# Stick-breaking attention on one Trainium2 core: the suffix sums of log keeps as two passes of rounded fp32 in place of one of plain fp32

## The chip, the cores and the metric

One core of one Trainium2 chip runs the whole program. The metric is device time in microseconds (us), the lower the better. The kernel before takes 2057.86 us (median of 3 runs, 2056.94 to 2059.09).

## The reference, cut to what matters

The program computes four transformer layers of 256 tokens and width 1024. Each layer is an FFN, a mixer and another FFN. The mixers are one retention, one latent attention (MLA) and two of the kind that the change touches, here called stick sublayers (the last two layers). A stick mixer projects the token rows to q, k, v (8 heads of 64), three convolution inputs and one pooling input, and its attention is

```python
z = einsum('bhqd,bhkd->bhqk', q_blk, kh) * scale
mask = k_pos[None, :] < q_pos[:, None]
log_keep = where(mask, log_sigmoid(-z), 0.0)
between = cumsum(log_keep, axis=3, reverse=True) - log_keep
a = where(mask, exp(log_sigmoid(z) + between), 0.0)
out = einsum('bhqk,bhkd->bhqd', a, vh)
```

Since log_sigmoid(z) = z + log_sigmoid(-z), the exponent is z plus the suffix sum of the log keeps, the key's own included: that sum is what the kernel forms on TensorE.

## The kernel before, in words

**Weights.** All projections read weights through a ring of three slots of 128x2048 fp32 (1 MB). SyncE loads slot n when `low(n-3)` is done. ScalarE's `high(n)` rounds it into `w_hi` (L881), and VectorE's `low(n)` puts the remainder into `w_lo` (L1197). TensorE then makes three matmuls of type fp32r (rounded fp32) per 128x128 tile: high by high, high by low, low by high (L400 to L402; L473 for the output projections). `high(n)` needs its slot loaded and `slot_done` of slot n-3; `low(n)` needs `high(n)`; TensorE's `take(n)` needs `low(n)`.

**Order.** There is no planner. Each engine has one list of instructions, written by hand, which it runs in order; what comes from another engine is waited for on a semaphore. An instruction that waits holds up all that stands behind it on its engine.

**Stick sublayer.** Ten weight slots (b to b+9) give q, k, v and the rest, and four give the output projection. The 8 heads go in 4 pairs s = 0 to 3. A pair's scores are kept transposed, keys on partitions; only the causal part stands, 384 columns per head (256 queries for the first 128 keys, 128 for the second). The steps of a pair, each with its engine:

- TensorE `pair_logits` (L731, L732): z in plain fp32 into the banks of `down[0]`.
- ScalarE `pair_log` (L1143, L1145, L1148): |z|, exp(-|z|), ln(1 + that).
- VectorE `pair_keep` (L1524, L1527): max(z, 0) plus that, then times the negated mask: `z_lk`, the log keeps of both heads, 128x768.
- TensorE `pair_sums` (L749 to L753), for each of two heads: z again for the first keys (L749), a triangle of ones times the log keeps on top (L750), all ones times those of the second keys (L751), and z and triangle for the second keys (L752, L753). All in plain fp32; each plain fp32 matmul stands as two instructions in the trace.
- VectorE `pair_min` (L1512), ScalarE `pair_exp` (L1131): the attention weights.
- TensorE `pair_out` (L763, L764), ScalarE `pair_high` (L1135), VectorE `pair_low` (L1517): the output, split for the next projection.

TensorE's list around them (L779 to L808): half of slot b+4, `pair_logits(0)`, the other half, slot b+5, `pair_sums(0)`, `pair_logits(1)`, slot b+6, `pair_out(0)`, half of slot b+7, `pair_sums(1)`, `pair_logits(2)`, the other half, `pair_out(1)`, slot b+8, `pair_sums(2)`, `pair_logits(3)`, slot b+9, `pair_out(2)`, `pair_sums(3)`, the pooling matmuls (L806), output projection. ScalarE's list is at L1150 to L1179 (`slot_out(j)` copies a projection out, L939) and VectorE's at L1530 to L1567. GpSimd makes the pooling sums (L1661 to L1666) at the same time. L513 and L438 are the transposes and the first matmuls after a sublayer's norm.

Of the kernel before, what the change touches and what calls it, by code (L numbers as in the profile page):

```python
# [17 lines left out]
P = 128  # L18
S = 256
# [15 lines left out]
CAUSAL = 384  # L35
# [62 lines left out]
def build(nc, ins, out):  # L98
# [3 lines left out]
    with ctx:  # L102
# [95 lines left out]
        sm = sb("sm", [P, 2, 2, 4])  # L198
        c_hi, c_lo = h_hi[:, 0:3, :], h_lo[:, 0:3, :]
        hgain = sb("hgain", [P, TOK])  # L200

        bank0, bank1 = ps("bank0", 512), ps("bank1", 512)
        down = [ps("down0", 1024), ps("down1", 1024)]
# [33 lines left out]
        c_turned, c_hi_done, c_lo_done = sem("c_turned"), sem("c_hi_done"), sem("c_lo_done")  # L237
        uq_mm, uq_out, ukv_mm, ukv_out = sem("uq_mm"), sem("uq_out"), sem("ukv_mm"), sem("ukv_out")
        qk_ready, qk_turned, qk_T = sem("qk_ready"), sem("qk_turned"), sem("qk_T")
        s_z, s_abs, s_ln, s_lk = sem("s_z"), sem("s_abs"), sem("s_ln"), sem("s_lk")  # L240
        s_cs, s_min, s_exp, s_out, s_hi, s_lo = (sem(n) for n in ("s_cs", "s_min", "s_exp", "s_out", "s_hi", "s_lo"))
        conv_done, conv_hi, conv_lo = sem("conv_done"), sem("conv_hi"), sem("conv_lo")
# [13 lines left out]
        def wait(eng, s, value):  # L256

            if value > 0:
                eng.wait_ge(s, value)
# [126 lines left out]
        def _(pe):  # L386
# [220 lines left out]
            for u, kind in enumerate(SUBLAYERS):  # L607
# [115 lines left out]
                else:  # L723
# [14 lines left out]

                    def pair_sums(s):

                        pe.wait_ge(s_lk, c0 + s + 1)
                        wait(pe, s_min, c0 + s)
                        tri, ones = cst("tri"), cst("ones")
                        for g in range(2):
                            o = 64 * g
                            k, q = s_k[o:o + 64, s, :], s_q[o:o + 64, s, :]
                            lk = z_lk[:, g, :]
                            first, second = mid[2 + g][:, 0:S], mid[2 + g][:, S:CAUSAL]
                            mm(first, k[:, 0:P], q, start=True, stop=False)  # L749
                            mm(first, tri, lk[:, 0:S], start=False, stop=False)  # L750
                            mm(mid[2 + g][:, P:S], ones, lk[:, S:CAUSAL], start=False, stop=True)  # L751
                            mm(second, k[:, P:S], q[:, P:S], start=True, stop=False)  # L752
                            last = mm(second, tri, lk[:, S:CAUSAL], start=False, stop=True)  # L753
                        last.then_inc(s_cs, 1)

                    def pair_out(s):
# [80 lines left out]
        def _(sc):  # L837
# [32 lines left out]
            def high(n, at=None, base=None):  # L870

                m = n if at is None else at
                if at is None:
                    sc.wait_ge(raw_in[n % RING], 16 * (n // RING + 1))
                    wait(sc, slot_done, n - RING + 1)
                else:
                    i, n0 = base
                    sc.wait_ge(raw_in[n0 % RING], i * 16 + 16 * (n0 // RING + 1))
                    sc.wait_ge(slot_done, m - RING + 1)
                r = n % RING  # L880
                act_fn(w_hi[:, r, :], raw[:, r, :], ACT.Copy).then_inc(hi_ready, 1)  # L881
# [109 lines left out]
            for u, kind in enumerate(SUBLAYERS):  # L991
# [44 lines left out]
                else:  # L1036
                    if kind == "ret":
                        mem = mem_heads(0)

                        def pair_high(p):  # L1040
                            sc.wait_ge(m_turned, p + 1)
                            act_fn(m_hi[:, 2 * p:2 * p + 2, :], (bank6, bank7)[p % 2][:, :].rearrange("p (k t) -> p k t", k=2),
                                   ACT.Copy).then_inc(m_hi_done, 1)
# [72 lines left out]
                    else:  # L1116
# [4 lines left out]
                        def slot_out(j):  # L1121
                            copy_out(b + j, places[j], scale=AD ** -0.5 if j in (2, 5) else 1.0)
# [14 lines left out]
                        def pair_log(s):  # L1137

                            sc.wait_ge(s_z, c0 + s + 1)
                            z = down[0][:, :].rearrange("p (a b) -> p a b", a=2)[:, :, 0:CAUSAL]  # L1140
                            if s:
                                sc.wait_ge(s_exp, c0 + s)
                            act_fn(z_abs, z, ACT.Abs).then_inc(s_abs, 1)  # L1143
                            sc.wait_ge(s_abs, 3 * (c0 + s) + 1)
                            act_fn(z_abs, z_abs, ACT.Exp, scale=-1.0).then_inc(s_abs, 1)  # L1145
                            sc.wait_ge(s_abs, 3 * (c0 + s) + 2)
                            wait(sc, s_lk, c0 + s)
                            act_fn(z_ln, z_abs, ACT.Ln, bias=1.0).then_inc(s_abs, 1)  # L1148

                        pair_log(0)  # L1150
                        slot_out(4)
                        high(b + 7)
                        slot_out(5)
                        high(b + 8)
# [1 line left out]
                        pair_log(1)  # L1156
                        slot_out(6)
                        pair_high(0)
                        high(b + 9)
                        pair_exp(1)  # L1160
                        pair_log(2)
                        slot_out(7)
                        high(b + 10)
                        pair_high(1)
                        slot_out(8)
# [2 lines left out]
                        pair_log(3)  # L1168
                        slot_out(9)
                        pair_high(2)  # L1170
                        high(b + 12)
                        pair_exp(3)
                        sc.wait_ge(small_in, SMALL_FIRST + SMALL_STICK * (sticks + 1))
                        sc.wait_ge(pool_mm, sticks + 1)
                        for j in range(2):
                            act_fn(m_hi[:, 6 + j, :], bank0[:, j * S:(j + 1) * S], ACT.Copy, scale=small[:, j, 3:4]).then_inc(pool_hi, 1)
                        sc.wait_ge(conv_done, 2 * (sticks + 1))
# [11 lines left out]
        def _(ve):  # L1189
            v = nc.vector  # L1190
# [16 lines left out]
            def pre_scale(p, t):  # L1207

                ve.wait_ge(pre_in, 16 * (p + 1))
                ve.wait_ge(pre_rs, 2 * p + t + 1)  # L1210
                for c in range(2):
                    h = slice(c * 512, (c + 1) * 512)
                    wait(ve, turned, 4 * (p - 1) + 2 * t + c + 1)
                    v.scalar_tensor_tensor(xn[:, t, h], (mem_rows if p == 0 else x)[:, t, h], stat[:, 4 + t:5 + t],  # L1214
                                           (post_gain if p == 0 else pre_gain)[:, h], ALU.mult, ALU.mult).then_inc(pre_xn, 1)
# [93 lines left out]

            for t in range(T):  # L1310
                pre_scale(0, t)
            pre_low(0, 0)
            low(0)
            low(1)
# [12 lines left out]
            for u, kind in enumerate(SUBLAYERS):  # L1327
# [47 lines left out]
                else:  # L1375
# [126 lines left out]
                    else:  # L1502
# [16 lines left out]
                        def pair_keep(s):  # L1519
# [7 lines left out]
                                last = v.tensor_tensor(z_lk[:, g, :], z_ln[:, g, :], cst("negmask"), ALU.mult)  # L1527
                            last.then_inc(s_lk, 1)

                        pair_keep(0)  # L1530
                        low(b + 7)
                        pair_min(0)
                        low(b + 8)
                        pair_keep(1)
                        pair_low(0)
                        pair_min(1)
                        low(b + 9)
                        pair_keep(2)
                        low(b + 10)
                        pair_low(1)  # L1540
                        pair_min(2)
                        low(b + 11)
                        pair_keep(3)
                        pair_low(2)

                        def convolve(j):

# [149 lines left out]
```

## Time and profile before

| what | value |
|---|---|
| median of 3 runs | 2057.86 us (2056.94 to 2059.09) |
| span of the profiled execution | 2058.1 us; no other time is listed for it |
| TensorE (PE) matmul busy | 1980.5 us, 96% |
| VectorE (DVE) busy | 1087.5 us, 53% |
| ScalarE (ACT) busy | 957.1 us, 47% |
| GpSimd (POOL) busy | 139.7 us, 7% |
| mean granted TensorE clock | 0.993 of full speed |
| DMA | 356.46 MB, mean 173 GB/s |

The span is one execution, from its first to its last instruction. Matmuls are pipelined, so successive starts, not the durations, say what one costs. A timeline row gives the start, the duration, the engine, the line and the count of merged instructions; the brackets give the idle time before it and what ended that.

### The profile page before, as it was taken

To read this page: it belongs to the slowest core of one execution; us is meant where nothing else is said; L and a number is where in the kernel's file an instruction comes from. 1 tells how busy PE (TensorE), PEld (TensorE's weight loads), DVE (VectorE), ACT (ScalarE), POOL (GpSimd) and SP (SyncE) were. 2 spreads that over 40 slices of the span, in tenths; PEclk is the share of its full clock that TensorE was granted. 3 is DMA by queue.
4 is the path that set the end of the run, shared out by engine and by line. 5 is a ranking of instruction groups with operands and counts; after the bars stand their busy time and mean duration, and the time that the engine had idled before them with its cause. 6 is when DMAs were issued, how large, how long until landed. Compare 5 with 4: busy or idle time off the path is not lost.

```text
span 2058.1 us, 32564 instructions
## 1 busy us (share of the span) xinstructions
PE 1980.5 (96%) x13724; PEld 1832.0 (89%) x13724; DVE 1087.5 (53%) x990; ACT 957.1 (47%) x1097; POOL 139.7 (7%) x149
## 2 busy tenths in 40 slices
PE   7999999999999998999999999999999999999998
PEld 6999899899899986899989998889998998988997
DVE  4644656644554456544564445554446445456444
ACT  5445554533543356533453346553445335555443
POOL 2500022000000000000000002000000000200000
PEclk9999999999999999999999999999999999999999
DMA  8655543555465542455555555355555554535552
GB/s 286 205 183 184 168 154 129 199 187 185 146 214 188 188 148 81 162 186 183 184 185 184 183 165 184 103 174 190 187 164 194 186 189 147 185 103 174 184 185 101
DMA packets 261987, 356.46 MB, mean 173 GB/s; under 512 B 8976, under 2 KB 230544, under 8 KB 261904
## 3 DMA queue, kind: packets, MB, share of 16 engines
q1 hardware_dynamic: 258304, 342.15, 50.4%
q0 software_dynamic: 3600, 13.11, 2.1%
q8 instruction: 63, 1.03, 0.2%
q14 instruction: 20, 0.16, 0.0%
HBM read 354.19 MB, written 1.05 MB: 173 GB/s over the span
## 4 chain that ended last, share of the span: by engine, by line
PE 87%; DVE 6%; issue 3%; ACT 3%; DMA 1%; POOL 0%; SPq 0%; DVEq 0%; POOLq 0%; ACTq 0%
PE down L473 24%; PE bank L400 17%; PE bank L402 17%; PE bank L401 17%; PE bank L447 2%; PE bank L513 2%; DVE upd L1234 2%; ACT junk L852 1%; PE bank L438 1%; PE bank L439 1%; DVE w_lo L1203 1%; DVE xn L1214 1%; DVE x L1240 1%; DMA raw<-in_ffn_w_gu 1%; PE down L749 0%
## 5 line engine op out<-in xcount | busy, mean ns | idle before, releaser
L1197 DVE TENSOR_TENSOR w_lo<-raw,w_hi 128x2048 fp32r<-128x2048 f32 x300 | 687.8, 2295 | 522.9 <-ACT w_hi L881 522.9
L400 PE MATMUL bank<-h_hi,w_hi 128*128 128x256 f32 x2944 | 835.6, 284 | 0.0
L401 PE MATMUL bank<-h_lo,w_hi 128*128 128x256 f32 x2944 | 833.0, 283 | 0.0
L402 PE MATMUL bank<-h_hi,w_lo 128*128 128x256 f32 x2944 | 833.0, 283 | 0.0
L881 ACT ACTIVATE w_hi<-raw 128x2048 fp32r<-128x2048 f32 x322 | 614.2, 1908 | 263.8 <-PE down L473 201.4
L400 PEld LDWEIGHTS bank<-h_hi,w_hi 128*128 128x128 f32 x2944 | 564.7, 192 | 6.4 <-issue 2.5
L401 PEld LDWEIGHTS bank<-h_lo,w_hi 128*128 128x128 f32 x2944 | 564.8, 192 | 2.5
L402 PEld LDWEIGHTS bank<-h_hi,w_lo 128*128 128x128 f32 x2944 | 564.8, 192 | 0.0
L473 PE MATMUL down<-w_hi,m_hi 128*128 128x512 f32 x832 | 267.2, 393 | 0.0
L473 PE MATMUL down<-w_lo,m_hi 128*128 128x512 f32 x832 | 264.7, 390 | 0.0
L473 PE MATMUL down<-w_hi,m_lo 128*128 128x512 f32 x832 | 264.4, 389 | 0.0
L473 PEld LDWEIGHTS down<-w_hi,m_lo 128*128 128x128 f32 x832 | 156.2, 188 | 33.2
L473 PEld LDWEIGHTS down<-w_lo,m_hi 128*128 128x128 f32 x832 | 156.3, 188 | 33.0
L1002 ACT ACTIVATE m_hi<-big 128x512 fp32r<-128x512 f32 x80 | 50.3, 629 | 287.8 <-DVE big L1336 287.8
L473 PEld LDWEIGHTS down<-w_hi,m_hi 128*128 128x128 f32 x832 | 151.2, 189 | 27.7 <-issue 1.4
L998 ACT ACTIVATE big<-bank 128x512 f32<-128x512 f32 x88 | 52.6, 598 | 250.2 <-PE bank L402 219.3
L1336 DVE TENSOR_TENSOR big<-bank,big 128x512 f32<-128x512 f32 x88 | 60.9, 692 | 144.6 <-PE bank L402 109.5
L1588 POOL TENSOR_TENSOR stat<-stat,const 128x1 f32<-128x1 f32 x24 | 14.4, 599 | 1506.7 <-ACT stat L863 1506.7
L438 PE MATMUL bank<-w_hi,h_hi 128*128 128x256 f32 x384 | 95.3, 286 | 12.5 <-issue 7.2
L439 PE MATMUL bank<-w_hi,h_lo 128*128 128x256 f32 x384 | 93.9, 282 | 0.0
L438 PEld LDWEIGHTS bank<-w_hi,h_hi 128*128 128x128 f32 x384 | 73.3, 191 | 16.7 <-issue 10.4
L513 PE MATMUL bank<-const,xn 128*128 128x128 f32 x208 | 36.9, 315 | 45.5 <-DVE xn L1214 45.4
(207 smaller groups left out, 1395.1 us busy)
## 6 DMA issues: line engine op xcount, KB each, us to landing
raw<-in_ffn_w_gu SPq DMA_DIRECT2D x88, 1024.0 KB, 5.1
raw<-in_ffn_w_down SPq DMA_DIRECT2D x88, 1024.0 KB, 4.9
raw<-in_ffn_w_gate SPq DMA_DIRECT2D x44, 1024.0 KB, 5.3
raw<-in_ffn_w_up SPq DMA_DIRECT2D x44, 1024.0 KB, 5.4
raw<-in_w_in SPq DMA_DIRECT2D x20, 1024.0 KB, 5.2
raw<-in_ret_w_in SPq DMA_DIRECT2D x13, 1024.0 KB, 5.7
raw<-in_w_o SPq DMA_DIRECT2D x8, 1024.0 KB, 5.0
raw<-in_w_out SPq DMA_DIRECT2D x8, 1024.0 KB, 4.9
```

Source lines behind the costliest of these rows:

```text
L400: mm(o, w_hi[:, r, c:c + P], hi[:, k, :], start=(k == 0), stop=False)
L401: mm(o, w_hi[:, r, c:c + P], lo[:, k, :], start=False, stop=False)
L402: last = mm(o, w_lo[:, r, c:c + P], hi[:, k, :], start=False, stop=(k == KD - 1))
L438: mm(o, hi[:, k, ts], w_hi[:, n % RING, c:c + SC], start=(k == 0), stop=False)
L439: mm(o, lo[:, k, ts], w_hi[:, n % RING, c:c + SC], start=False, stop=False)
L473: last = mm(down[t][:, c * 512:(c + 1) * 512], a[:, k0 + j, ts], w[:, r, j * D + c * 512:j * D + (c + 1) * 512], start=(first and j == 0 a ...
L513: last = tr((bank6, bank7)[c][:, k * P:(k + 1) * P], xn[:, t, (4 * c + k) * P:(4 * c + k + 1) * P], ident)
L881: act_fn(w_hi[:, r, :], raw[:, r, :], ACT.Copy).then_inc(hi_ready, 1)
L998: act_fn(silu_g, bank0[:, :], ACT.Silu).then_inc(silu_done, 1)
L1002: act_fn(m_hi[:, k0:k0 + 2, :], act.rearrange("p (a b) -> p a b", a=2), ACT.Copy).then_inc(act_hi_done, 1)
L1197: v.tensor_tensor(w_lo[:, r, :], raw[:, r, :], w_hi[:, r, :].bitcast(f32), ALU.subtract).then_inc(lo_ready, 1)
L1336: v.tensor_tensor(act, bank1[:, :], silu_g, ALU.mult).then_inc(prod_done, 1)
```

## The change

`pair_sums` gets its triangle and ones in fp32r (`tri_r`, `ones_r`, copied once at the start), and the log keeps as two fp32r tiles, a high part (`lk_hi`, a rounding copy) and a low part (`lk_lo`, the remainder), laid over rows 4 to 6 of `m_hi` and `m_lo`. Per head, the z matmuls stay in plain fp32; the triangle goes over all 384 columns at once, once with each part, and the ones over 128 columns, once with each part. ScalarE gets `keep_high(s)` and VectorE `keep_low(s)`, at the places below. The complete diff:

```diff
@@ build: tiles and semaphores
+        tri_r = sb("tri_r", [P, P], f32r)
+        ones_r = sb("ones_r", [P, P], f32r)
+        lk_hi = m_hi[:, 4:7, :].rearrange("p a b -> p (a b)").rearrange("p (a b) -> p a b", a=2)
+        lk_lo = m_lo[:, 4:7, :].rearrange("p a b -> p (a b)").rearrange("p (a b) -> p a b", a=2)
+        s_lk_hi, s_lk_lo, exact_ready = sem("s_lk_hi"), sem("s_lk_lo"), sem("exact_ready")
@@ TensorE
                     def pair_sums(s):
 
-                        pe.wait_ge(s_lk, c0 + s + 1)
+                        pe.wait_ge(s_lk_lo, c0 + s + 1)
                         wait(pe, s_min, c0 + s)
-                        tri, ones = cst("tri"), cst("ones")
+                        pe.wait_ge(exact_ready, 2)
                         for g in range(2):
                             o = 64 * g
                             k, q = s_k[o:o + 64, s, :], s_q[o:o + 64, s, :]
-                            lk = z_lk[:, g, :]
-                            first, second = mid[2 + g][:, 0:S], mid[2 + g][:, S:CAUSAL]
-                            mm(first, k[:, 0:P], q, start=True, stop=False)
-                            mm(first, tri, lk[:, 0:S], start=False, stop=False)
-                            mm(mid[2 + g][:, P:S], ones, lk[:, S:CAUSAL], start=False, stop=True)
-                            mm(second, k[:, P:S], q[:, P:S], start=True, stop=False)
-                            last = mm(second, tri, lk[:, S:CAUSAL], start=False, stop=True)
+                            z = mid[2 + g][:, 0:CAUSAL]
+                            mm(z[:, 0:S], k[:, 0:P], q, start=True, stop=False)
+                            mm(z[:, S:CAUSAL], k[:, P:S], q[:, P:S], start=False, stop=False)
+                            for lk in (lk_hi, lk_lo):
+                                mm(z, tri_r[:, :], lk[:, g, :], start=False, stop=False)
+                            for part, lk in enumerate((lk_hi, lk_lo)):
+                                last = mm(z[:, P:S], ones_r[:, :], lk[:, g, S:CAUSAL], start=False, stop=(part == 1))
                         last.then_inc(s_cs, 1)
@@ ScalarE
+                        def keep_high(s):
+                            sc.wait_ge(s_lk, c0 + s + 1)
+                            wait(sc, s_cs, c0 + s)
+                            act_fn(lk_hi, z_lk, ACT.Copy).then_inc(s_lk_hi, 1)
+
                         pair_log(0)
                         slot_out(4)
+                        keep_high(0)
                         high(b + 7)
                         slot_out(5)
                         high(b + 8)
@@
                         pair_log(1)
                         slot_out(6)
                         pair_high(0)
+                        keep_high(1)
                         high(b + 9)
                         pair_exp(1)
                         pair_log(2)
                         slot_out(7)
+                        keep_high(2)
                         high(b + 10)
                         pair_high(1)
                         slot_out(8)
@@
                         pair_log(3)
                         slot_out(9)
                         pair_high(2)
+                        keep_high(3)
                         high(b + 12)
                         pair_exp(3)
                         sc.wait_ge(small_in, SMALL_FIRST + SMALL_STICK * (sticks + 1))
                         sc.wait_ge(pool_mm, sticks + 1)
+                        sc.wait_ge(s_cs, c0 + 4)
@@ VectorE, at the start
                 pre_scale(0, t)
+            ve.wait_ge(const_in, 16)
+            v.tensor_copy(tri_r[:, :], cst("tri")).then_inc(exact_ready, 1)
+            v.tensor_copy(ones_r[:, :], cst("ones")).then_inc(exact_ready, 1)
             pre_low(0, 0)
@@ VectorE
+                        def keep_low(s):
+                            ve.wait_ge(s_lk_hi, c0 + s + 1)
+                            v.tensor_tensor(lk_lo, z_lk, lk_hi.bitcast(f32), ALU.subtract).then_inc(s_lk_lo, 1)
+
                         pair_keep(0)
                         low(b + 7)
+                        keep_low(0)
                         pair_min(0)
                         low(b + 8)
                         pair_keep(1)
                         pair_low(0)
+                        keep_low(1)
                         pair_min(1)
                         low(b + 9)
                         pair_keep(2)
                         low(b + 10)
+                        keep_low(2)
                         pair_low(1)
                         pair_min(2)
                         low(b + 11)
                         pair_keep(3)
                         pair_low(2)
+                        keep_low(3)
```

## Rows read from the trace of the kernel before

**Rows 1.** The page's first part and the chain's shares by engine.
```profile
PE 1980.5 (96%) x13724; PEld 1832.0 (89%) x13724; DVE 1087.5 (53%) x990; ACT 957.1 (47%) x1097; POOL 139.7 (7%) x149
...
PE 87%; DVE 6%; issue 3%; ACT 3%; DMA 1%; POOL 0%; SPq 0%; DVEq 0%; POOLq 0%; ACTq 0%
```

**Rows 2.** The waits of TensorE: for what, us in total, times, longest.
```profile
PE down L749 <- DVE big L1527: 0.9, 2, 0.4
```

**Rows 3.** Timeline of TensorE in the first stick sublayer: pair 0, later starts.
```profile
1277.88 0.28 PE L402 MATMUL bank<-h_hi,w_lo 128*128 128x256 f32 x1
1278.09 0.70 PE L749 MATMUL down<-big 64*128 64x256 f32 x2
1278.72 0.70 PE L750 MATMUL down<-big,const 128*128 128x256 f32 x2
1279.25 0.38 PE L751 MATMUL down<-big,const 128*128 128x128 f32 x2
1279.57 0.49 PE L752 MATMUL down<-big 64*128 64x128 f32 x2
1279.98 0.49 PE L753 MATMUL down<-big,const 128*128 128x128 f32 x2
1280.40 0.70 PE L749 MATMUL down<-big 64*128 64x256 f32 x2
...
1282.71 0.71 PE L731 MATMUL down<-big 64*128 64x256 f32 x4
...
1283.57 0.39 PE L400 MATMUL bank<-h_hi,w_hi 128*128 128x256 f32 x1
...
1293.39 0.48 PE L749 MATMUL down<-big 64*128 64x256 f32 x1
...
1308.68 0.48 PE L749 MATMUL down<-big 64*128 64x256 f32 x1
...
1321.42 0.70 PE L749 MATMUL down<-big 64*128 64x256 f32 x2 [0.44 <-DVE big L1527]
```

**Rows 4.** Timeline of TensorE in the MLA sublayer: fp32r matmuls of 384 columns.
```profile
780.31 0.34 PE L417 MATMUL bank<-w_lo,h_hi 128*128 128x384 f32 x1
780.48 0.33 PE L418 MATMUL bank<-w_hi,h_lo 128*128 128x384 f32 x1
```

**Rows 5.** Timeline of VectorE in the first stick sublayer.
```profile
1275.62 1.73 DVE L1527 TENSOR_TENSOR big<-big,const 128x384 f32<-128x384 f32 x2
1277.27 2.28 DVE L1197 TENSOR_TENSOR w_lo<-raw,w_hi 128x2048 fp32r<-128x2048 f32 x1
...
1298.12 1.02 DVE L1512 SCALAR_TENSOR_TENSOR big<-down,const 128x384 f32<-128x384 f32 x2 [6.82 <-PE down L753]
...
1305.05 1.03 DVE L1527 TENSOR_TENSOR big<-big,const 128x384 f32<-128x384 f32 x2
...
1321.80 0.68 DVE L1556 TENSOR_TENSOR big<-big 128x512 f32<-128x512 f32 x1
```

**Rows 6.** Timeline of ScalarE in the first stick sublayer.
```profile
1274.91 1.90 ACT L881 ACTIVATE w_hi<-raw 128x2048 fp32r<-128x2048 f32 x1
...
1299.17 0.85 ACT L1131 ACTIVATE big<-big 128x768 f32<-128x768 f32 x1 [5.24 <-DVE big L1512]
...
1321.05 0.38 ACT L1135 ACTIVATE m_hi<-bank 128x256 fp32r<-128x256 f32 x1 [0.23 <-PE bank L764]
```

**Rows 7.** Timeline of TensorE at the program's start.
```profile
15.63 0.58 PE L438 MATMUL bank<-w_hi,m_hi 128*128 128x256 f32 x1 [2.48 <-ACT w_hi L881]
```

**Rows 8.** Busy time by stretch; columns: length, PE, PEld, DVE, ACT, POOL, PEclk, DMA, GB/s.
```profile
1241.00:1243.00 2.00, 0.45 (x4) 0.25 (x3) 0.99 (x1) 1.84 (x6) 0.54 (x2) 1.00 0.57 198
...
1244.00:1247.00 3.00, 3.00 (x15) 3.00 (x16) 2.80 (x4) 1.38 (x3) 0.53 (x1) 0.50 0.67 232
```

**Rows 9.** Timeline of GpSimd in the first stick sublayer.
```profile
1277.36 3.08 POOL L1662 TENSOR_TENSOR big<-big 128x508 f32<-128x508 f32 x1
...
1281.11 1.03 POOL L1662 TENSOR_TENSOR big<-big 128x504 f32<-128x504 f32 x1
```

## The prediction

> **What bounds the kernel now.** I read the page first: TensorE is busy 96% of the span and holds 87% of the chain that ended last [rows 1]. Then TensorE's waits: in both stick sublayers together it waits for the log keeps only 0.9 us, in two places [rows 2]. So any TensorE time taken out of `pair_sums` comes out of the end, and any wait put before it is added to the end. Then the timeline of one sublayer on three engines, because each runs its own list in order, and the change puts two steps into two lists and a new releaser before `pair_sums`.
>
> Pair 0's sums start at 1278.09, right behind the last matmul of slot b+5 [rows 3]. The log keeps they need were done at 1275.62 + 1.73 = 1277.35 [rows 5]: a slack of 0.7 us. The sums take 1282.71 - 1278.09 = 4.62 us and `pair_logits(1)` 0.86 us [rows 3].
>
> **What the change saves on TensorE.** Per head the old sums take 2.31 us (1278.09 to 1280.40), by successive starts 0.63, 0.53, 0.32, 0.41 and 0.42 [rows 3]. Their columns, each at four passes and 2.4 GHz, would be 4 x 896 / 2.4 = 1.49 us; the four passes are my reading, by which L750's 256 columns (0.43) fit in its 0.53. The other 0.82 us lies between the matmuls, about 0.1 to 0.2 each, more where the number of rows goes from 64 to 128 or back. An fp32r matmul of 384 columns goes at 0.17 us (780.31 to 780.48) [rows 4], so it takes one pass. New per head: z over 384 columns in plain fp32 0.64, change to 128 rows 0.2, triangle 2 x 0.17, ones 2 x 0.12 (the nearest rate is that of the 256-column L400 to L402: 48 of them in the 5.8 us of a slot), change back to 64 rows 0.2: 1.62, for two heads 3.25. No row shows an fp32r matmul of 128 columns. Below, columns alone: 4 x 384 + 2 x 384 + 2 x 128 = 2560 columns, 1.07 us per head, 2.13 per pair; with the changes of rows 2.9. Above: 128 columns cost what L751's two instructions do, 0.32 [rows 3], twice: 3.25 + 2 x 2 x 0.20, about 4.0. I take 3.3, nearest to the widths that rows show. Eight pairs (two sublayers) x 1.32 = **10.6 us saved**, bounds 5 and 14.
>
> What hides nothing is the order of the lists, so I work out each pair's wait. Durations: a `high` 1.90 [rows 6], a `low` 2.28 [rows 5]. `keep_high` is a ScalarE pass over 128x768, as L1131: 0.85 [rows 6]. `keep_low` lies between VectorE's 0.68 for 512 columns and 2.28 for 2048 [rows 5]: 0.95. About 0.05 us goes by at each hand-over.
>
> **Pair 0.** `keep_high(0)` stands ahead of `high(b+7)` in ScalarE's list and must wait for the log keeps at 1277.35; before, that `high` ran from 1274.91 [rows 6]. Now: `keep_high` to 1278.25, `high(b+7)` to 1280.2. On VectorE `low(b+7)` stands ahead of `keep_low(0)`, and needs that `high`: to 1282.5; `keep_low` to 1283.45. TensorE is there at 1278.09: **5.4 us of waiting**, with everything behind it held: logits 1, slot b+6 and all the rest of the program.
>
> **Pair 1.** From the end of one pair's sums to the next pair's log keeps is 8.07 us: sums 1 end at 1293.39 + 4.62 = 1298.01, L1512 starts at 1298.12, L1527 ends at 1306.08 [rows 3, 5]. `pair_high(0)` stands before `keep_high(1)`; TensorE ends `pair_out(0)` 7.6 us after the sums (0.86, a slot 5.86, 0.9), L1135 takes 0.38 [rows 6], so `keep_high(1)` runs from 8.2 to 9.05 and `keep_low(1)` to 10.05. TensorE comes back to the sums after 1293.39 - 1282.71 = 10.68 [rows 3]. The work that hides the two steps is slot b+6 and half of b+7, with 0.6 us left over: **0**.
>
> **Pair 2.** Log keeps at 8.07, `keep_high(2)` 8.95, then `high(b+10)` 10.85, `low(b+10)` 13.2, `keep_low(2)` 14.2. TensorE is back after 1308.68 - 1298.01 = 10.67 [rows 3]: **3.5 us of waiting**.
>
> **Pair 3.** `pair_high(2)` holds `keep_high(3)` to 8.2; `keep_low(3)` ends at 10.05. TensorE is back after 1321.42 - 0.44 - (1308.68 + 4.62) = 7.68 [rows 3]: 2.4 us of waiting, 0.44 of which stands already [rows 2, 3]: **+1.95**.
>
> Sum per sublayer 5.4 + 3.5 + 1.95 = 10.9, two sublayers **21.8 us added**. These sums don't hang on the length of the new `pair_sums`, since each chain starts where the sums end.
>
> **TensorE's clock.** In the stretch 1241 to 1243 TensorE was busy 0.45 of 2 us, and in 1244 to 1247 its clock was granted at 0.50, 1.2 GHz [rows 8]. The 5.4 us wait is longer than that pause, the other two about as long. One fall costs at most 1.5 us of the 3 us it lasts, and part of it lies inside the wait. I take two falls per sublayer at 1.0 us: **+4**, bounds 0 and 10 (three falls per sublayer at 1.65).
>
> **Costed at nothing.** The two copies at the start (128x128, some 0.2 us each) delay `pre_low(0, 0)`; TensorE's next matmul waits for ScalarE until 15.63, at the end of 2.48 us of idleness [rows 7], which hides them. The new wait before the pooling copies is for sums that TensorE has already run when it does pooling. The tiles over `m_hi` and `m_lo` are not in use in that stretch. DMAs: none added; the ring's later loads start as much later as the `low` that releases them, and the slot after next is used over 10 us on. The low slots after the sublayer shift along with it.
>
> **Sum.** 21.8 - 10.6 + 4 = +15.2. The profiled span, 2058.1, lies 0.2 above the median of 2057.86, so I add to the median: **2073.1 us**, slower by 0.74%.
>
> One rule of the Trainium skill is set against the rows here. The rows show gaps of 0.1 to 0.2 us between plain fp32 matmuls, which the change also removes. The Trainium skill ("TensorE: Matmul & The Clock Gate", Back-to-back issue gap) gives an isolated warm matmul N/2.4 plus 2.5 ns. If only columns counted, a pair would go from 2.99 to 2.13, a saving of 0.85, 6.8 us over eight pairs, and the time would be 2076.9. The trace disagrees with it for these instructions, 2.31 against 1.5 per head, so I keep to the rows.
>
> **Rivals.**
>
> A, the sums win as much as the waits cost: `pair_sums` runs at the rate of its columns, 2.13 us a pair, and the clock never falls. It saves 8 x 2.49 = 19.9 and ends at 2057.9 + 21.8 - 19.9 = 2059.8, the same within the bound. Deciding point: below 2.4 us a pair the change is no longer slower than the bound; at 1.9 it breaks even. For it: z of the two heads overlaps in `pair_logits`, 0.86 us where 1.28 stands by columns. Against it: in `pair_sums` 128-row matmuls stand between the heads, and the changes of rows cost 0.2. Chance 4%; faster 1%.
>
> B, every wait drops the clock: three falls per sublayer at 1.65 make 9.9 in place of 4: 2079. For it: 0.45 busy of 2 us was enough once [rows 8]. Against: part of each half-speed stretch lies in the wait. Chance 17%.
>
> C, narrow fp32r matmuls are slow: 128 columns of them cost as plain fp32. The pair takes 4.0, the saving 5.0: 2078.7. Nothing in the rows speaks for or against. Chance 20%.
>
> D, VectorE and GpSimd block each other at `keep_low(0)`. L1662 took 3.08 us beside `low(b+7)` and 1.03 elsewhere [rows 9], and L1527's pair 1.73 in place of 1.03 [rows 5]. `keep_low(0)` now falls in the pooling work; if a pooling step gets in first, it waits up to 1.03 us in each sublayer: 2075. Against: `low` and `keep_low` follow without a gap, and at 1277.27 VectorE kept GpSimd out that way. The Trainium skill ("SBUF — State Buffer", SBUF: two separate sides) says the port pair is locked for a whole instruction by whoever starts first; the trace agrees. Chance 9%.
>
> E, the change is not what it says: the fp32r matmuls on the same banks cost as much as before. Then only the waits stand: 2083. Rows 4 speak against. Chance 2%.
>
> My forecast, with sizes near those taken, has 48%.
>
> **How the numbers follow.** The range goes from the short sums with few falls (2.9 us a pair, clock +1.5: 21.8 - 13.8 + 1.5 = 9.5, 2067) to B or C with some of the other (+22.5, 2080.5). Below lies A, above B and C together with D. About 0.2% (4.1 us) is what a measurement of this kernel can tell from no change. Slower by more: all but A, 95%; same 4%; faster 1%.
>
> **What would show it.** In the changed kernel's profile TensorE should wait before L749's successor for `keep_low` about 5.4, 0, 3.5 and 2.4 us, near 22.6 in both sublayers; `high(b+7)` and `high(b+10)` should start right behind the `keep_high` before them; the sums should take 3.3 us from first start to the next logits; the clock should be 0.50 in some 3 us after the first wait. The prediction is wrong if VectorE runs `keep_low` before `low(b+7)` has waited, if the sums take under 2.4 or over 4.2 us, or if the waits fall on pair 1.

## The result and the profile after

The changed kernel takes 2083.61 us (median of 4 runs, 2081.94 to 2085.93) beside 2058.48 us for the kernel before on the same chip: a ratio of 1.0124, 95% interval 1.0110 to 1.0139, so 25 us slower. The direction and the waits were forecast; 2073.1 us and the range up to 2080.5 were too low. The span of the profiled execution went from 2058.1 to 2080.8 us.

The page of the changed kernel, first part and chain by engine, answers to [rows 1]:

```profile
PE 1981.8 (95%) x13692; PEld 1836.8 (88%) x13692; DVE 1094.8 (53%) x1000; ACT 963.1 (46%) x1105; POOL 137.0 (7%) x149
...
PE 85%; DVE 7%; issue 3%; ACT 3%; DMA 1%; POOL 0%; SPq 0%; DVEq 0%; POOLq 0%; ACTq 0%
```

TensorE's waits, the row that takes the place of [rows 2] (us in total, times, longest):

```profile
PE down L753 <- DVE m_lo L1550: 21.5, 6, 5.3
```

L753 is the first z matmul of `pair_sums`, L1550 is `keep_low`. Six waits, three per sublayer, 21.5 us; 0.9 us stood there before. They come about as worked out: `high(b+7)` (L886) starts right behind `keep_high(0)` (L1158) on ScalarE, and `low(b+7)` (L1212) waits for it ahead of `keep_low(0)` on VectorE.

```profile
1273.92 0.85 ACT L1158 ACTIVATE m_hi<-big 128x768 fp32r<-128x768 f32 x1 [2.37 <-DVE big L1545]
1274.67 1.89 ACT L886 ACTIVATE w_hi<-raw 128x2048 fp32r<-128x2048 f32 x1
```
```profile
1276.60 2.29 DVE L1212 TENSOR_TENSOR w_lo<-raw,w_hi 128x2048 fp32r<-128x2048 f32 x1 [2.71 <-ACT w_hi L886]
1278.81 1.15 DVE L1550 TENSOR_TENSOR m_lo<-big,m_hi 128x768 fp32r<-128x768 f32 x1
```

The timeline of TensorE in the first stick sublayer, pairs 0, 1, 2 and 3 in turn, answers to [rows 3]:

```profile
1280.01 1.22 PE L753 MATMUL down<-big 64*128 64x256 f32 x2 [5.31 <-DVE m_lo L1550]
1281.03 0.63 PE L754 MATMUL down<-big 64*128 64x128 f32 x2
1281.59 0.69 PE L756 MATMUL down<-m_hi,tri_r 128*128 128x384 f32 x1
1282.08 0.52 PE L756 MATMUL down<-m_lo,tri_r 128*128 128x384 f32 x1
...
1285.68 1.23 PE L736 MATMUL down<-big 64*128 64x256 f32 x4
...
1287.27 0.58 PE L405 MATMUL bank<-h_hi,w_hi 128*128 128x256 f32 x1
...
1298.83 0.70 PE L753 MATMUL down<-big 64*128 64x256 f32 x2
1299.36 0.38 PE L754 MATMUL down<-big 64*128 64x128 f32 x2
1299.67 0.45 PE L756 MATMUL down<-m_hi,tri_r 128*128 128x384 f32 x1
1299.96 0.34 PE L756 MATMUL down<-m_lo,tri_r 128*128 128x384 f32 x1
1300.14 0.22 PE L758 MATMUL down<-m_hi,ones_r 128*128 128x128 f32 x1
1300.20 0.27 PE L758 MATMUL down<-m_lo,ones_r 128*128 128x128 f32 x1
1300.40 0.70 PE L753 MATMUL down<-big 64*128 64x256 f32 x2
...
1301.96 0.71 PE L736 MATMUL down<-big 64*128 64x256 f32 x4
...
1315.96 1.22 PE L753 MATMUL down<-big 64*128 64x256 f32 x2 [3.24 <-DVE m_lo L1550]
...
1321.62 1.23 PE L736 MATMUL down<-big 64*128 64x256 f32 x4
...
1333.21 0.70 PE L753 MATMUL down<-big 64*128 64x256 f32 x2 [2.22 <-DVE m_lo L1550]
...
1336.74 2.02 PE L811 MATMUL bank<-big,pool_w 128*128 128x256 f32 x4
```

Two things are to be seen. The waits are 5.31, none, 3.24 and 2.22 us. And the same `pair_sums` takes 3.13 us for pair 1 (1298.83 to 1301.96) but 5.67 us for pair 0 and 5.66 for pair 2, each matmul in it almost twice as long. The granted clock says why (changed kernel, busy time by stretch; columns: length, PE, PEld, DVE, ACT, POOL, PEclk, DMA, GB/s):

```profile
1277.00:1281.00 4.00, 0.99 (x2) 0.83 (x3) 2.96 (x2) 3.13 (x3) 3.94 (x3) 0.58 0.23 40
1281.00:1284.00 3.00, 3.00 (x10) 2.44 (x9) 0.00 (x0) 0.00 (x0) 2.78 (x4) 0.50 0.72 296
1284.00:1287.00 3.00, 3.00 (x15) 2.50 (x13) 1.21 (x3) 0.15 (x1) 0.37 (x1) 0.50 0.00 0
1287.00:1291.00 4.00, 4.00 (x21) 3.77 (x20) 2.01 (x1) 3.85 (x5) 0.00 (x0) 0.50 0.19 32
1291.00:1295.00 4.00, 4.00 (x35) 3.87 (x33) 2.05 (x4) 0.62 (x1) 0.00 (x0) 0.97 0.58 235
```

The clock falls in the wait, at 1277.6, and is 0.50 (1.2 GHz) until 1291.2, though TensorE is busy without a gap from 1280.0 on. Behind the pause of [rows 8] it was back after 1247. Each of the three waits of a sublayer has a fall, in it or within 1.1 us behind it. Behind pairs 2 and 3 of the first sublayer and pair 0 of the second:

```profile
1316.00:1325.00 9.00, 9.00 (x32) 7.56 (x33) 3.46 (x4) 2.66 (x4) 0.00 (x0) 0.50 0.35 117
1336.00:1339.00 3.00, 3.00 (x10) 2.54 (x10) 1.95 (x5) 0.96 (x2) 0.00 (x0) 0.50 0.00 0
...
1797.00:1806.00 9.00, 7.81 (x26) 6.38 (x27) 3.17 (x5) 2.20 (x4) 5.25 (x6) 0.50 0.29 117
```

The same clock over the whole sublayer, 1255 to 1340, in the kernel before and in the changed one:

```profile
1255.00:1340.00 85.00, 84.56 (x579) 73.36 (x578) 43.57 (x51) 50.01 (x50) 13.55 (x14) 1.00 0.39 127
```
```profile
1255.00:1340.00 85.00, 74.23 (x478) 67.43 (x477) 38.43 (x49) 48.88 (x51) 12.15 (x14) 0.84 0.33 108
```

**Where the time went, first sublayer.** From where TensorE was ready for pair 0's sums to the start of `pair_out(3)`, the kernel before takes 1332.37 - 1278.09 = 54.3 us and the changed one 1344.38 - (1280.01 - 5.31) = 69.7 us: +15.4. The waits are 10.77 us, 0.44 of them old: +10.3. The sums at full clock save 4 x (4.62 - 3.13) = 6.0. That leaves 11.1 us for the clock. Piece by piece, 10.8 of them can be found: pair 0's sums +2.5, its logits +0.7, some 17 matmuls of slot b+6 at 0.21 in place of 0.12 +1.6; pair 2's sums +2.5, logits and slot b+9 behind them +1.8; from pair 3 to the first projection matmuls some +1.7.

The second sublayer, by the same starts, takes 67.2 us in place of 54.3: +12.9, of which 8.6 us are the clock's. Over the whole program, by the ratio: 25.1 = 20.6 (21.5 less 0.9) - 11.9 (eight pairs at 1.49) + 16.4, with an interval of some 3 us either way. The two sublayers alone give 19.7. Part of the difference is that the profiled execution of the kernel before lost about 5 us to falls in the MLA sublayer (0.94 over 790 to 870, where the changed kernel has 1.00), which have nothing to do with the change.

### The profile page after: what moved, and what is told of

Read it like the earlier page. It is cut to its first block, busy times and chain, and to the rows that moved or that the text cites. A ratio compares the mean times of both kernels' runs of the same rounds, so it can differ in the third digit from the quotient of the medians.

```text
span 2080.8 us, 32526 instructions
## 1 busy us (share of the span) xinstructions
PE 1981.8 (95%) x13692; PEld 1836.8 (88%) x13692; DVE 1094.8 (53%) x1000; ACT 963.1 (46%) x1105; POOL 137.0 (7%) x149
## 4 chain that ended last, share of the span: by engine, by line
PE 85%; DVE 7%; issue 3%; ACT 3%; DMA 1%; POOL 0%; SPq 0%; DVEq 0%; POOLq 0%; ACTq 0%
PE down L478 23%; PE bank L405 17%; PE bank L406 16%; PE bank L407 16%; PE bank L452 2%; PE bank L518 2%; DVE upd L1249 2%; ACT junk L857 1%; PE bank L443 1%; PE bank L444 1%; DVE w_lo L1218 1%; DVE xn L1229 1%; DVE w_lo L1212 1%; PE down L753 1%; DVE x L1255 1%
## 5 line engine op out<-in xcount | busy, mean ns | idle before, releaser
L1212 DVE TENSOR_TENSOR w_lo<-raw,w_hi 128x2048 fp32r<-128x2048 f32 x300 | 687.6, 2294 | 533.5 <-ACT w_hi L886 533.5
L886 ACT ACTIVATE w_hi<-raw 128x2048 fp32r<-128x2048 f32 x322 | 614.2, 1908 | 267.5 <-PE down L478 201.4
L1003 ACT ACTIVATE big<-bank 128x512 f32<-128x512 f32 x88 | 52.6, 598 | 245.9 <-PE bank L407 216.2
L443 PEld LDWEIGHTS bank<-w_hi,h_hi 128*128 128x128 f32 x384 | 73.6, 192 | 16.7 <-issue 10.4
L1358 DVE TENSOR_TENSOR m_lo<-big,m_hi 128x512 fp32r<-128x512 f32 x80 | 55.3, 691 | 44.6 <-ACT m_hi L1007 44.6
```

The costliest lines, as they stand in the source:

```text
L443: mm(o, hi[:, k, ts], w_hi[:, n % RING, c:c + SC], start=(k == 0), stop=False)
L1003: act_fn(silu_g, bank0[:, :], ACT.Silu).then_inc(silu_done, 1)
L1212: v.tensor_tensor(w_lo[:, r, :], raw[:, r, :], w_hi[:, r, :].bitcast(f32), ALU.subtract).then_inc(lo_ready, 1)
L1358: v.tensor_tensor(m_lo[:, k0:k0 + 2, :], act.rearrange("p (a b) -> p a b", a=2), m_hi[:, k0:k0 + 2, :].bitcast(f32), ALU.subtract).then_in ...
```

## The experiments

Theory 1 was that the clock costs those 16 us; theory 2 that it costs the 4 us forecast and the new matmuls or steps the rest. The kernels are edits of the changed kernel. Beside these experiments the kernel before took 2054.0 to 2063.3 us, so the ratios, taken on the same chip, count more than the medians.

### The old sums behind the new waits

```diff
@@ pair_sums
-                        pe.wait_ge(exact_ready, 2)
+                        tri, ones = cst("tri"), cst("ones")
                         for g in range(2):
...
-                                mm(z, tri_r[:, :], lk[:, g, :], start=False, stop=False)
+                            mm(first, tri, lk[:, 0:S], start=False, stop=False)
...
```

> The changed kernel with the old plain fp32 matmuls in pair_sums, which read z_lk but still wait for keep_low. Theory 1 (three terms: waits of about 10.8 us per sublayer, 12 us saved by the new sums, and some 16 us lost because the TensorE clock stays at 0.50 long after each wait): the waits stay at 5.3, 0, 3.2 to 3.5 and 2.2 to 2.4 us, the saving goes, and the low clock costs at least as much as before: about 2058.5 + 20.6 + 16 = 2095 us. Theory 2 (the new matmuls themselves are what costs the rest, the clock only the 4 us forecast): 2058.5 + 20.6 + 4 = 2083 us.

2109.92 us, ratio 1.0256 (1.0237 to 1.0275): +53 us. TensorE's waits are as before, six of them, 21.6 us. Theory 2 is out by 27 us: without any new matmul, 32 us are lost beyond the waits (0.0256 of 2056 is 52.6, less 20.7). Theory 1's own number was 15 us low: I had kept the clock's price at 16, and with the longer sums more work runs slowly: behind pair 3 of the first sublayer the clock is 0.50 for 10 us, where it was for 3 in the changed kernel. Pair 0's sums take 8.34 us at the low clock:

```profile
1285.99 1.22 PE L754 MATMUL down<-big 64*128 64x256 f32 x2 [5.31 <-DVE m_lo L1550]
...
1294.33 1.23 PE L736 MATMUL down<-big 64*128 64x256 f32 x4
```

### Filling the waits

```diff
+                    def fill(bank, n):
+                        for i in range(n):
+                            mm(bank[:, 0:S], h_hi[:, i % KD, 0:P], h_hi[:, (i + 1) % KD, :], start=(i == 0), stop=(i == n - 1))
                     def pair_sums(s):
...
+                        fill((bank6, bank7)[s % 2], {0: 40, 1: 0, 2: 24, 3: 14}[s])
                         pe.wait_ge(s_lk_lo, c0 + s + 1)
```

> The changed kernel with filler matmuls (fp32r, 256 columns, into a bank that the next pair_out overwrites) ahead of the waits of pairs 0, 2 and 3: 40, 24 and 14 of them, 0.12 us each, so they end before the wait does. No wait gets shorter. Theory 1 (the low clock): the clock stays at 1.00 through both sublayers, the sums take 3.1 us for every pair, and the time is 2058.5 + 20.6 - 12 = 2067 us. Theory 2 (the clock costs only some 4 us): 2080 us.

2066.31 us, ratio 1.0053 (1.0034 to 1.0073): +10 us where the changed kernel has +25. The lines left out make the fillers of pairs 2 and 3 wait until `pair_low` has read their bank. They are useless and no step comes earlier; they only keep TensorE busy through the waits. By TensorE's waits 2.7 us are left, and over the sublayer the clock is 1.00:

```profile
PE down L762 <- DVE m_lo L1559: 2.7, 6, 0.5
```
```profile
1255.00:1340.00 85.00, 83.67 (x607) 76.36 (x606) 44.58 (x54) 51.62 (x53) 12.16 (x14) 1.00 0.36 121
```

By the ratios 0.0071 of 2057 us came back, 14.6 us; that is the clock's price, shown by itself, and the two intervals together (0.0014 and 0.0020) leave it open by some 5 us either way. What is left, +10, is about the waits less the saving: 20.6 - 11.9 = 8.7.

The same fillers ahead of the old plain sums (the two edits together) isolate the saving:

> The kernel waits_old_sums with the same fillers as filled_waits (40, 24, 14). Both keep the clock up, so their difference is the plain saving of the new sums: eight pairs at 4.62 less 3.13 us, 12 us. Theory 1: 2066.3 + 12 = 2078 us, and the clock is not below 1.00 in the sublayers. A theory by which the new matmuls save more or less than their starts say would give another difference.

2081.01 us, ratio 1.0108 (1.0089 to 1.0127). Against the filled new sums, which ran on another chip, that is 0.0055 of 2057, 11.3 us, with intervals of 0.0019 on each side, together some 5 us either way: in keeping with the 12 us that successive starts gave, though it could not tell 12 from 10.

### The steps without the wait

```diff
@@ the kernel waits_old_sums, pair_sums
-                        pe.wait_ge(s_lk_lo, c0 + s + 1)
+                        pe.wait_ge(s_lk, c0 + s + 1)
```

> keep_high and keep_low stand in their lists as in the change, but TensorE runs the old plain sums from z_lk behind the old wait. This takes the releaser away from the critical path and leaves the work of the two steps, and the later low(b+7) and low(b+10). Theory 1 (the steps cost by TensorE's wait alone): the time of the kernel before, within 1 us. Rival: the later high and low steps or the start copies cost by themselves: up to 4 us more.

2056.39 us, ratio 0.9994 (0.9983 to 1.0006), which allows at most 1.2 us. `keep_high`, `keep_low`, the later `high` and `low` of slots b+7 and b+10 and the two copies at the start cost nothing that can be measured. The term costed at nothing was right.

### What holds the clock down

First I suspected plain fp32 work. The runs of this section are single executions, one profile each. Their times are rough; the granted clock can be read at two waits in each of two sublayers. The first puts 16 fp32r fillers on 128 rows behind the waits of pairs 0 and 2:

```diff
@@ pair_sums, fp32r_behind_wait
                         pe.wait_ge(exact_ready, 2)
...
+                        fill((bank6, bank7)[s % 2], {0: 16, 1: 0, 2: 16, 3: 0}[s])
```

> The changed kernel with 16 fp32r filler matmuls of 256 columns between the wait and the first z matmul, for pairs 0 and 2. What is asked is what holds the clock down for 10 to 14 us. Theory 1a (plain fp32 work does not bring the clock back, fp32r work does): the low stretch behind pair 0 and pair 2 gets shorter, to 7 us or less, and the sums run at 3.1 us. Theory 1b (the length depends on the wait alone): the stretches stay at 13.7 and 10.2 us, and the time grows by 4 x 16 x 0.21 = 14 us.

2099.9 us, one run: +42. Theory 1a fell as put: the sums of pair 0 still ran at half speed and the clock was 0.50 from the wait until past 1293. Theory 1b had it right here: the low stretches of the first sublayer kept their 13.7 and 10.2 us, and the time is some 17 us more above the kernel before than the changed kernel's, where it gave 14.

```profile
1281.00:1285.00 4.00, 3.77 (x17) 3.54 (x17) 0.18 (x1) 0.37 (x1) 3.78 (x5) 0.50 0.82 262
1285.00:1293.00 8.00, 8.00 (x28) 6.56 (x28) 2.28 (x3) 1.13 (x2) 0.60 (x1) 0.50 0.01 2
```

The second leaves z out of the exponent:

```diff
@@ pair_sums, no_z_in_sums
-                            mm(z[:, 0:S], k[:, 0:P], q, start=True, stop=False)
-                            mm(z[:, S:CAUSAL], k[:, P:S], q[:, P:S], start=False, stop=False)
                             for lk in (lk_hi, lk_lo):
-                                mm(z, tri_r[:, :], lk[:, g, :], start=False, stop=False)
+                                mm(z, tri_r[:, :], lk[:, g, :], start=(lk is lk_hi), stop=False)
```

> The changed kernel without the two plain fp32 z matmuls in pair_sums (z is left out of the exponent). Per pair 1.3 to 1.6 us less at full clock, eight pairs 11 to 13 us. Theory 1a: with less plain fp32 behind the wait the clock comes back one step sooner, so another 3 to 8 us go: 2062 to 2068 us. Theory 1b: the low stretches stay at 13.7 and 10.2 us: 2070 us.

2058.4 us, one run. The waits stay at 21.6 us. The time is below both numbers given, in the direction of theory 1a. Behind pair 0's wait (it ends at 1278.6) the clock is back at 1286.4, after 7.8 us, where the changed kernel needs 11.2; the averages over 1255 to 1340 are 0.92 and 0.84. Theory 1b has fallen too: the wait is the same and the stretch is not. The z matmuls, plain fp32 on 64 rows, thus matter to the clock, but this edit takes away the type, the 64 rows and the changes of rows at once. Four more kernels put one kind of long filler each behind the waits of pairs 0 and 2:

```diff
@@ long_fp32r_behind
+                            mm(bank[:, 0:S], h_hi[:, i % KD, 0:P], h_hi[:, (i + 1) % KD, :], start=(i == 0), stop=(i == n - 1))
@@ long_plain_behind
+                            mm(bank[:, 0:S], cst("tri"), z_lk[:, i % 2, 0:S], start=(i == 0), stop=(i == n - 1))
@@ long_64row_behind
+                            mm(bank[:, 0:S], s_k[0:64, s, 0:P], s_q[0:64, s, :], start=(i == 0), stop=(i == n - 1))
@@ long_alternating_behind
+                            a, m = ((s_k[0:64, s, 0:P], s_q[0:64, s, :]), (cst("tri"), z_lk[:, 0, 0:S]))[i % 2]
+                            mm(bank[:, 0:S], a, m, start=(i == 0), stop=(i == n - 1))
```

The first has n = 48, the others n = 12.

> As fp32r_behind_wait, but 48 fp32r fillers (5.8 us at full clock, 10 us at half) behind the waits of pairs 0 and 2. Theory 1a (fp32r work brings the clock back, the plain fp32 sums do not): the clock is back at 1.00 within the fillers, the sums of pairs 0 and 2 take 3.1 us, and the low stretches are 10 us or shorter. Theory 1b (the length depends on the wait alone, 13.7 and 10.2 us whatever follows): the clock comes back 13.7 us after its fall, and the sums of pair 0 run in part at half.

> The same with 12 plain fp32 fillers of 256 columns, which by columns at four passes have the same TensorE time as 48 fp32r ones. Theory 1a: the clock stays at 0.50 through the fillers and the sums behind them, some 10 us longer than in the changed kernel (23 us behind pair 0). Theory 1b: it comes back 13.7 us after its fall, within fillers or sums.

> As long_plain_behind, with 12 plain fp32 fillers on 64 rows (the pair's own k and q) in place of 128 rows. Theory 2a (work on 64 rows does not bring the clock back): it stays at 0.50 through the fillers and the sums behind them, over 20 us behind pair 0. Theory 2b (it is the gaps where the number of rows changes, not the rows): with fillers of one shape the clock is back within them, as with the 128-row ones, after some 7 us.

> As long_plain_behind, but the 12 fillers alternate between 64 and 128 rows, so that each has a gap of 0.1 to 0.2 us beside it at full clock. Theory 2b (the gaps hold it down): the clock stays at 0.50 through them and the sums. Theory 2a (64-row work counts little): it may come back late, after 10 us or more, since half the fillers are on 128 rows.

The times, one run each: 2103.38, 2100.38, 2122.42 and 2137.95 us. Busy time by stretch, first for the fp32r fillers on 128 rows (they start at 1278.89), then for the plain ones on 128 rows (1280.02):

```profile
1279.00:1283.00 4.00, 4.00 (x19) 4.00 (x20) 0.00 (x0) 0.03 (x1) 3.78 (x4) 0.50 0.65 251
1284.00:1288.00 4.00, 4.00 (x30) 3.69 (x29) 0.00 (x0) 0.00 (x0) 0.00 (x0) 1.00 0.01 4
```
```profile
1280.00:1285.00 5.00, 4.98 (x12) 4.01 (x13) 0.00 (x0) 0.16 (x1) 4.12 (x5) 0.50 0.55 206
1286.00:1290.00 4.00, 4.00 (x20) 3.21 (x19) 0.00 (x0) 0.00 (x0) 0.00 (x0) 1.00 0.00 0
```

With both kinds the clock comes back while they run, at 1283.3 (4.4 us after they begin) and at 1285.4 (5.3 us), and the sums behind them run at full speed. At the other three places it takes 3.1 to 5.1 and 3.4 to 4.4 us. So the number type is not it; theory 1a fell for good with long_plain_behind, and so did 1b. Then the 64-row fillers (from 1281.43) and the alternating ones (from 1279.93):

```profile
1280.00:1290.00 10.00, 8.57 (x20) 6.79 (x21) 1.38 (x2) 1.55 (x2) 5.48 (x6) 0.50 0.33 105
1290.00:1299.00 9.00, 9.00 (x30) 7.10 (x29) 1.55 (x3) 0.50 (x1) 0.00 (x0) 0.50 0.01 2
1301.00:1305.00 4.00, 4.00 (x36) 4.00 (x35) 1.65 (x4) 2.25 (x3) 0.00 (x0) 1.00 0.74 262
```
```profile
1280.00:1290.00 10.00, 10.00 (x18) 4.42 (x18) 0.00 (x0) 0.07 (x1) 4.04 (x4) 0.50 0.27 103
1290.00:1302.00 12.00, 12.00 (x35) 8.33 (x35) 2.49 (x3) 1.35 (x2) 0.00 (x0) 0.50 0.00 1
```

Matmuls on 64 rows do not bring it back: the fillers run without a gap from 1281.43 to 1291.84, 10.4 us, at 0.50 all the way, the sums and logits behind them too, and the clock returns at 1300.5, once the matmuls of slot b+6 run (128 rows, 256 columns). The other three places agree; behind pair 2 of the first sublayer:

```profile
1328.00:1344.00 16.00, 16.00 (x48) 12.81 (x48) 2.61 (x3) 1.47 (x2) 0.00 (x0) 0.50 0.12 50
```

These fillers have one shape and no change of rows among them, so changes of rows are not needed (theory 2a). Against the plain ones on 128 rows they differ in the rows and in the data that they read (k and q in place of triangle and log keeps); no run changed the data alone. The alternating ones, half of them on 128 rows, don't bring it back either: the clock returns at 1302.4. Whether that is their 64-row half or the gaps beside each was not told apart.

### The steps at better places

```diff
@@ ScalarE
                         slot_out(4)
-                        keep_high(0)
                         high(b + 7)
+                        keep_high(0)
...
                         pair_log(3)
+                        keep_high(3)
                         slot_out(9)
                         pair_high(2)
-                        keep_high(3)
@@ VectorE
                         pair_keep(0)
-                        low(b + 7)
                         keep_low(0)
+                        low(b + 7)
...
                         pair_keep(2)
-                        low(b + 10)
                         keep_low(2)
+                        low(b + 10)
...
                         pair_keep(3)
-                        pair_low(2)
                         keep_low(3)
+                        pair_low(2)
```

> The changed kernel with the new steps at other places of the lists: keep_low right behind pair_keep for pairs 0, 2 and 3, high(b+7) ahead of keep_high(0), keep_high(3) ahead of slot_out(9) and pair_high(2). Theory 1: the waits fall to about 1.1, 0, 0 and 2.2 us, and with no long wait the clock falls rarely: 2058.5 + 5.7 - 12 = 2052 us, up to 2056 if a fall follows pair 3. Theory 2 (the new matmuls cost the rest): 2058.5 + 5.7 + 4 = 2068 us.

2058.61 us (10 runs, 2055.93 to 2062.54), ratio 1.0014 (1.0004 to 1.0023). The waits came out close to what was worked out:

```profile
PE down L753 <- DVE m_lo L1550: 6.8, 4, 2.3
```

Four waits, 1.1 and 2.3 us per sublayer. Yet the time is 2.4 us above the kernel before (2056.24 beside it), where theory 1 had 6.5 below, or 2.5 below with a fall. So some 9 us are lost beyond waits and saving (0.0014 of 2056, plus 11.9, less 5.9 of new waits). The profile has four falls in the two sublayers. Even 1.12 us of idleness ahead of pair 0's sums (1273.31 to 1274.42) was followed by one, while the sums ran:

```profile
1273.00:1277.00 4.00, 2.88 (x16) 2.25 (x15) 3.36 (x2) 3.98 (x4) 3.88 (x4) 1.00 0.00 0
1277.00:1280.00 3.00, 3.00 (x14) 2.50 (x15) 1.98 (x3) 0.89 (x2) 2.81 (x5) 0.51 0.70 206
```

Next TensorE does 2.7 us of the output projection ahead of pair 3's sums:

```diff
@@ order, TensorE
                     pair_out(2)
+                    pe.wait_ge(s_lo, c0 + 2)
+                    pe.wait_ge(s_lk, c0 + 4)
+                    take(b + N_STICK)
+                    down_of(b + N_STICK, 0, 0, m_hi, m_lo, True, False)
                     pair_sums(3)
...
-                gemm_down(b, 2 * WO_ORDER[kind][0], True, second=second)
+                if kind == "stick":
+                    second()
+                    down_of(b, 0, 1, m_hi, m_lo, True, False).then_inc(slot_done, 1)
+                else:
+                    gemm_down(b, 2 * WO_ORDER[kind][0], True, second=second)
```

> As order, and TensorE does the first token tile of output projection slot b+10 (2.7 us) ahead of pair_sums(3), after waiting for pair_keep(3), whose bank it writes. Theory 1: the 2.2 us wait of pair 3 becomes about 0.4 us, and after the pooling matmuls some 0.4 us for pair_min(3): 2058.5 + 2 x (1.1 + 0.8 - 0.44) - 12 = 2049.5 us, faster than both kernels. Theory 2 (the new matmuls cost the rest): above 2060 us.

> The kernel order_pe once more, beside order_pe_filled on the same chip, with more rounds, to place it against the kernel before. Its terms: waits +2.9 us over both sublayers, sums -12, a fall of the clock or two +2: -7 us, a ratio of 0.9965.

2053.68 us, ratio 0.9988 (0.9974 to 1.0002) the first time, which is not told from no change; 2053.15 us, 0.9980 (0.9967 to 0.9994) the second: 2.5 to 4 us faster than the kernel before, where 9 and 7 were expected. In the 12 runs of the second it took 2047.49 to 2062.38 us. Pair 0's 1.1 us is the wait that is left, so the last kernel puts 8 fillers into it, `fill(bank6, 8)` for s = 0:

> order_pe with 8 fp32r fillers (1 us) in the 1.1 us wait of pair 0, which is the largest left. Theory 1: the clock stays up through pair 0, 1 to 2 us per sublayer less than order_pe (2053.7 beside 2056.2 for the kernel before): 0.997 of the kernel before, 2051 us. If the fall at pair 0 does not come from the wait, it equals order_pe.

2049.05 us (6 runs, 2045.04 to 2051.42), ratio 0.9953 (0.9939 to 0.9967), beside order_pe's 0.9980 on the same chip: 5.6 us, some 4 either way, for 16 useless matmuls of 0.12 us. It is faster than both kernels, by about 9 us and by some 35. It has no wait before the sums that the view lists. The clock fell behind pair 0's 1.1 us in both sublayers of all three profiles without fillers (order, order_pe, order_pe_again), and in neither with them; order_pe and order_pe_filled:

```profile
1274.00:1284.00 10.00, 8.88 (x52) 7.75 (x51) 7.20 (x5) 7.81 (x8) 9.61 (x9) 0.83 0.29 107
```
```profile
1274.00:1284.00 10.00, 9.85 (x73) 9.00 (x72) 8.19 (x6) 7.60 (x9) 9.63 (x10) 1.00 0.28 107
```

## Why the prediction was wrong

**The saving**: right. 3.3 us a pair was taken, 3.13 measured at full clock; 10.6 us forecast, 11.9 by starts, 11.3 by the two filled kernels. The row that was missing, fp32r at 128 columns, came out at the low end: 1300.14 to 1300.20 is 0.06 us, one pass. Rivals A, C and E are out by the 3.13; that the time came out near E's 2083 is chance, since E had the sums save nothing. The Trainium skill ("TensorE: Matmul & The Clock Gate", Back-to-back issue gap) gives 0.056 us for an isolated gap at that width, and about 0.081 us in a stream of weight loads and matmuls; the 0.06 here is near the first, which did not hold for the plain fp32 group.

**The waits**: right, and each at its place. Forecast 5.4, 0, 3.5 and 2.4, measured 5.31, 0, 3.24 and 2.22; 21.8 us forecast for both sublayers, 20.6 measured. `keep_high` took 0.84 and `keep_low` 0.95 us, as taken.

**Rival D**: in small at most. Pair 0's `keep_low` took 1.15 us in both sublayers, and 0.95 to 0.96 is the usual: 0.2 us per sublayer.

**TensorE's clock**: the step that failed. The prediction has "I take two falls per sublayer at 1.0 us: +4, bounds 0 and 10 (three falls per sublayer at 1.65)". It counted two falls where the profile has three per sublayer, priced a fall by the one pause of [rows 8], some 3 us at half speed, and took for granted that the work behind a wait brings the clock back as fast as the work behind that pause did. There, transposes and matmuls on 128 rows followed. Behind these waits stand the sums, with their 64-row z matmuls, and the next logits on 64 rows. Behind pair 0 the clock stayed at 0.50 for 13.6 us in the first sublayer, 11.2 of them with TensorE busy, and for 10.2 us in the second, 8.5 of them busy. The term measured 14.6 us by the filled kernel and 16.4 by the balance, above the bound of 10. Rival B named the right mechanism, and its 9.9 us had the same mistaken length. With 14.6 in place of 4, and the other terms as they stood, the sum is 2057.9 + 21.8 - 10.6 + 14.6 = 2083.7. That it hits the 2083.6 so closely is luck: with the waits and the saving as measured the sum is 20.6 - 11.9 + 14.6 = +23.3, where +25.1 was measured, inside what the intervals allow.

A second omission: I held that the waits don't hang on the sums' length. They don't, but the slow clock is not hidden in the next wait either: pair 3's wait is 2.22 us in the changed kernel and 2.2 with the long 64-row fillers ahead of it. `pair_high(2)` stands ahead of `keep_high(3)` and waits for `pair_out(2)`, so a slow slot b+9 delays the very step that TensorE then waits for.

## What to carry to other kernels

When a step is put into a list that runs in order, work out the time at which it can start from what stands ahead of it; for pairs 0 and 2 the greater part of the wait here was not the 0.85 and 0.95 us of the steps but a `high` and a `low` that TensorE had to sit through; reordering the lists alone took the waits from 21.5 to 6.8 us. Price a wait on TensorE as the wait plus the slow clock behind it, and read the length of that from what work follows: in the profiles here every rise in a stick sublayer came while a matmul on 128 rows ran, such as one of slot b+6 at 1291.2 in the changed kernel. Count the 64-row work ahead of such matmuls at half speed. Where a short wait cannot be removed, filling it with useless matmuls can be worth more than the wait itself: 5.6 us for two waits of 1.1 here.

## What the runs showed of the hardware that I had not expected

- Matmuls on 64 rows, though TensorE was busy with them for 10.4 us on end, were not followed by a rise of the granted clock from 0.50, at any of four places; with the long fillers on 128 rows, fp32r or plain fp32, it rose 3.1 to 5.3 us after they began, at all eight. The shorter run of sixteen fp32r fillers behind pair 0 (3.7 us) ended at 0.50, and so did the sums behind it.
- In the kernel before, the same 64-row work at full clock, with no wait ahead of it, never lost the clock in the first sublayer (1.00 over 1255 to 1340); with 1.1 us of idleness ahead it fell at all six places in the profiles of order, order_pe and order_pe_again. Keeping a clock and getting it back are not the same question, and these runs don't say where the line lies.
- Filling 1.1 us of idleness twice gave back 5.6 us (0.9980 to 0.9953), and the falls behind it were gone.
